# Scores over all 128 rows, sums of the first and last up units made in DRAM, and 192 keys and queries for 256 in the first mixer's tiles

## The reference, cut to what matters

```python
proj = rms_norm(h) @ w_in              # q, k, v of mixer A (16 heads, 4 kv heads) and of mixer B (16 heads)
# mixer A: a 64-token chunk of queries sees its own chunk of keys and the one before (window 128),
#          with a fixed bias by distance and one learned sink logit a head
# mixer B: a chunk sees its own and the 8 before it (here: every earlier token), with a learned bias
sc = einsum(qc, kb) * dh ** -0.5 + bias;  p = softmax(sc);  o = einsum(p, vb)      # dh = 64
h = h + (sigmoid(gates_a) * (att_a @ w_branch_a) + sigmoid(gates_b) * (att_b @ w_branch_b)) @ w_out
u = square(relu(rms_norm(h) @ w_mlp_in))          # w_mlp_in: 2048 x 8192
h = h + u @ w_mlp_out                             # w_mlp_out: 8192 x 2048
out = rms_norm(h)
```

## Time and profile before

| | us |
|---|---|
| median of three runs (2509.68 to 2511.41) | 2510.68 |
| the profiled execution | 2511.8 |
| its span, first to last instruction | 2510.0 |
| PE busy | 2483.1 (99%) |
| PE weight loads busy | 2186.5 (87%) |
| DVE busy | 1674.0 (67%) |
| ACT busy | 1024.6 (41%) |
| POOL busy | 195.6 (8%) |

### The profile page before, as it was taken

One profiled execution on the slowest core, in us unless ns is written; L12 is line 12 of the kernel. 1 busy time (PEld: TensorE's weight loads), 2 busy tenths in 40 slices (PEclk: granted clock), 3 DMA queues, 4 the chain that ended last, 5 costly groups with the idle time before them and its releaser, 6 DMA issues.

```text
span 2510.0 us, 34657 instructions
## 1 busy us (share of the span) xinstructions
PE 2483.1 (99%) x14226; PEld 2186.5 (87%) x14226; DVE 1674.0 (67%) x2280; ACT 1024.6 (41%) x1316; POOL 195.6 (8%) x178
## 2 busy tenths in 40 slices
PE   9999999999999999999999999999999999999998
PEld 8898888888888888878899999999997888888886
DVE  5566555556333332524688888888889888877897
ACT  5455654456222222312444333333335444444445
POOL 0000000000101000001200000000011011110010
PEclk9999999999999999999999999999999999999999
DMA  7777777777889989842233434334348666566652
GB/s 258 212 214 193 216 195 200 215 200 214 235 253 245 266 239 253 259 150 93 76 126 127 134 127 135 127 131 138 128 158 331 230 227 212 197 229 234 228 192 109
DMA packets 192225, 483.54 MB, mean 193 GB/s; under 512 B 13104, under 2 KB 117696, under 8 KB 182224
## 3 DMA queue, kind: packets, MB, share of 16 engines
q1 hardware_dynamic: 180672, 347.26, 41.2%
q0 software_dynamic: 11264, 134.23, 21.4%
q10 hardware_dynamic: 144, 0.02, 0.0%
HBM read 460.44 MB, written 155.23 MB: 245 GB/s over the span
## 4 chain that ended last, share of the span: by engine, by line
PE 95%; DVE 2%; DMA 2%; POOL 1%; issue 0%; ACT 0%; SPq 0%; DVEq 0%; POOLq 0%; ACTq 0%
PE bank L1576 30%; PE bank L1578 30%; PE bank L1577 30%; PE bank L1654 2%; PE bank L1683 1%; PE bank L1666 1%; DMA landing<-in_w_out 1%; POOL raw_forms L1473 0%; DMA landing<-in_w_in 0%; DVE form_lo_b L1257 0%; DMA raw_forms<-hidden_rows 0%; DVE at_lo L1144 0%; DVE up_lo L1289 0%; PE bank L1583 0%; DMA up_raw<-in_up_units 0%
## 5 line engine op out<-in xcount | busy, mean ns | idle before, releaser
L941 DVE TENSOR_TENSOR w_lo<-landing,w_hi 128x1024 fp32r<-128x1024 f32 x200 | 248.8, 1244 | 469.7 <-ACT w_hi L613 469.3
L613 ACT ACTIVATE w_hi<-landing 128x1024 fp32r<-128x1024 f32 x200 | 212.1, 1060 | 626.3 <-PE bank L1578 612.5
L824 ACT ACTIVATE up_hi<-up_raw 128x1792 fp32r<-128x1792 f32 x128 | 218.1, 1704 | 413.1 <-PE bank L1578 392.3
L1576 PE MATMUL bank<-xn_hi,w_hi 128*128 128x512 f32 x928 | 367.0, 395 | 3.1 <-DVE w_lo L941 2.5
L871 ACT ACTIVATE ring<-down_raw 128x1024 fp32r<-128x1024 f32 x224 | 237.5, 1061 | 310.7 <-PE bank L1578 310.7
L1578 PE MATMUL bank<-xn_hi,w_lo 128*128 128x512 f32 x928 | 361.8, 390 | 0.0
L1577 PE MATMUL bank<-xn_lo,w_hi 128*128 128x512 f32 x928 | 361.4, 389 | 0.0
L1370 DVE TENSOR_TENSOR ring<-down_raw,ring 128x1024 fp32r<-128x1024 f32 x224 | 285.4, 1283 | 68.2 <-ACT ring L871 68.2
L1289 DVE TENSOR_TENSOR up_lo<-up_raw,up_hi 128x1792 fp32r<-128x1792 f32 x128 | 262.2, 2048 | 75.7 <-ACT up_hi L824 75.7
L1576 PE MATMUL bank<-ring,down_forms 128*128 128x512 f32 x656 | 255.4, 389 | 2.4 <-DVE ring L1370 2.4
L1576 PE MATMUL bank<-form_hi_b,up_hi 128*128 128x256 f32 x896 | 254.0, 283 | 3.5 <-DVE up_lo L1289 3.5
(11 more groups left out here) (180 smaller groups left out, 4809.4 us busy)
## 6 DMA issues: line engine op xcount, KB each, us to landing
down_totals<-in_down_blocks POOLq DMA_DIRECT2D x64, 1024.0 KB, 8.7
up_raw<-in_up_units SPq DMA_DIRECT2D x128, 512.0 KB, 3.4
down_raw<-down_totals SPq DMA_DIRECT2D x128, 512.0 KB, 4.5
down_raw<-in_down_blocks SPq DMA_DIRECT2D x96, 512.0 KB, 4.3
landing<-in_w_in SPq DMA_DIRECT2D x72, 512.0 KB, 5.8
landing<-in_w_gate SPq DMA_DIRECT2D x64, 512.0 KB, 6.0
landing<-in_w_out SPq DMA_DIRECT2D x32, 512.0 KB, 3.7
hidden_rows<-hidden_out SPq DMA_DIRECT2D x32, 512.0 KB, 3.4
```

Of the source, the lines that this page charges most:

```text
L613: nc.scalar.activation(w_hi[:, u % SPLIT, :], landing[:, u % LAND, :], ACT.Copy).then_inc(unit_hi, 1)
L824: nc.scalar.activation(up_hi[n % 2], up_raw[n % 3][:, 1:8, :], ACT.Copy).then_inc(up_hi_done, 1)
L941: nc.vector.tensor_tensor(w_lo[:, s, :], landing[:, u % LAND, :], w_hi[:, s, :].bitcast(F32), ALU.subtract).then_inc(unit_lo, 1)
L1576: nc.tensor.matmul(dst, a_hi, b_hi, start=start, stop=False, **kw)
```

## The change

**1. Scores.** The low queries are doubled like the high ones, and both groups of `scores` run over 128 rows (the product low by low comes with it). `double_q` makes four copies for two, waits for `proj_ready` (the low queries, made by DVE) in place of `proj_hi`, and there is one buffer for both parts in place of two buffers of the high part.

**2. Tiles of mixer A.** A 128-query tile sees 192 keys: tile t > 0 takes keys 128t - 64 to 128(t+1). `scores`, the bias step, the exponential and the normalising work on 192 for 256. `turn_probs` still turns two blocks of 128 (the unseen 64 columns are zeroed once). `times_v` multiplies each key block with 192 queries for 256.

**3. Up sums.** For the first eight and the last eight up units the sums are made in DRAM, by two more steps of `totals` (18 for 16), which run first; the first ten steps follow each other by 8 units for 10. SP loads the four ready blocks of such a unit with a second DMA of 512 KB, in rows of 1 KB. `up_sums` on POOL is gone, and on DVE for these units.

In the diff `UP_END` is 8 and `UP_UNITS` 128.

```diff
+def summed_in_dram(n):
+    return n < UP_END or n >= UP_UNITS - UP_END
...
 def head_tiles(h):
-
+    if h < A_HEADS:
+        places = ((4, 0), (4, P), (5, 0), (5, 2 * P))
+        return [(max(0, t * P - CHUNK), P + CHUNK * (t > 0), *places[t], 2 * P * t - (P - CHUNK) * (t > 0))
+                for t in range(TT)]
...
+def turned_keys(h, t):
+
+    return P * (1 + (t > 0)) if h < A_HEADS else P * (t + 1)
...
+        def q_parts(h):
+            return (q_hi[:, 0, :], q_lo[:, 0, :]) if h >= HEADS - 4 else (q_twice[:, 0, :], q_twice[:, 1, :])
...
+                if summed_in_dram(n):
+                    end = int(n >= UP_END)
+                    if n in (0, UP_UNITS - UP_END):
+                        sp.wait_ge(totals_added, 16 * 4 * (end + 1))
+                    sums = up_totals[end, :, :, n - end * (UP_UNITS - UP_END), :]
+                    sp.dma_start(up_raw[n % 3][:, 4:8, :], sums.rearrange("b p n -> p b n"))\
+                        .then_inc(up_landed[n % 3], 16)
...
             def double_q(h):
-                act.wait_ge(proj_hi, ready_count(block_no("q", mixer, g)))
-                if h >= 2:
-                    act.wait_ge(scores_done, h - 1)
+                act.wait_ge(proj_ready, ready_count(block_no("q", mixer, g)))
+                if h:
+                    act.wait_ge(scores_done, h)
                 r, qb = q_place(h)
-                nc.scalar.activation(q_twice(h)[0:DH], q_hi[r:r + DH, qb, :].bitcast(F32), ACT.Copy)
-                nc.scalar.activation(q_twice(h)[DH:P], q_hi[r:r + DH, qb, :].bitcast(F32), ACT.Copy).then_inc(q_doubled, 1)
+                for twice, part in zip(q_parts(h), (q_hi, q_lo)):
+                    for half in range(2):
+                        ins = nc.scalar.activation(twice[half * DH:(half + 1) * DH], part[r:r + DH, qb, :].bitcast(F32), ACT.Copy)
+                ins.then_inc(q_doubled, 1)
...
             def up_high(n):
-                if n in (1, 2, 3):
-                    act.wait_ge(up_summed_first, 3 * n)
+                if summed_in_dram(n):
+                    act.wait_ge(up_landed[n % 3], up_landings(n))
                 else:
-                    act.wait_ge(up_summed, 3 if n == 0 else 3 * (n - 2))
+                    act.wait_ge(up_summed, 3 * (n - UP_END) + 3)
...
-                if n + 2 < UP_UNITS:
+                if not summed_in_dram(min(n + 2, UP_UNITS - 1)):
                     up_sums(n + 2)
...
-            for m in range(STEPS):
-                pool.wait_ge(unit_used, 12 + 10 * m)
+            for m in range(2 + STEPS):
+                pool.wait_ge(unit_used, 12 + 8 * m if m < 10 else 84 + 10 * (m - 9))
...
             def scores(h):
-                for rows, query in ((slice(0, P), q_twice(h)), (slice(r, r + DH), q_lo[r:r + DH, qb, :])):
+                for k, query in enumerate(q_parts(h)):
                     for t, (first, n, bk, col, _) in enumerate(head_tiles(h)):
                         ins = nc.tensor.matmul(bank[:, bk, col:col + n], query[:, t * P:(t + 1) * P],
-                                               keys[rows, first * P:first * P + n],
-                                               start=col == 0 and query.shape[0] == P, stop=query.shape[0] == DH,
+                                               keys[:, first:first + n], start=col == 0 and k == 0, stop=k == 1,
                                                skip_group_check=True)
```

More of the change, by code:

```diff
@@ L40 @@
             + [(SUBS - 2 + s, v) for s, v in IN_TURN])
+UP_END = len(IN_TURN)
 UP_FORM = (0, 3, 5, 1, 4, 2, 6)
@@ L87, in up_place, with up_landings @@
     return UP_ORDER.index((s, v))
+def summed_in_dram(n):
+    return n < UP_END or n >= UP_UNITS - UP_END
+def up_landings(n):
+    return 16 * sum(2 if summed_in_dram(k) else 1 for k in range(n % 3, n + 1, 3))
 def form_places():
@@ L302, in q_place, with turned_part @@
             return hh % 2 * DH, 2 * (g % 2) + hh // 2
+        def turned_part(part, h, t):
+            if h >= A_HEADS:
+                return part[:, t, 0:P * (t + 1)]
+            if t == 0:
+                return part[:, 0:1, 0:P]
+            at = 512 * (t - 1) + P
+            return part[:].rearrange("p t n -> p (t n)")[:, at:at + 768].rearrange("p (b n) -> p b n", n=384)[:, :, 0:P]
         def block_parts(c):
@@ L682, in turned_probs @@
                     act.wait_ge(pt_done, TT * h + bank_end(h, t))
-                    nc.scalar.activation(pt_hi[:, t, first * P:first * P + n], bank[:, bk, col:col + n], ACT.Copy)\
+                    turned = bank[:, bk, col:col + turned_keys(h, t)]
+                    if h < A_HEADS:
+                        turned = turned.rearrange("p (b n) -> p b n", n=P)
+                    nc.scalar.activation(turned_part(pt_hi, h, t), turned, ACT.Copy)\
                         .then_inc(pt_hi_done, 1)
@@ L1074, in turned_probs @@
                     dve.wait_ge(pt_hi_done, TT * h + bank_end(h, t))
-                    nc.vector.tensor_tensor(pt_lo[:, t, first * P:first * P + n], bank[:, bk, col:col + n],
-                                            pt_hi[:, t, first * P:first * P + n].bitcast(F32), ALU.subtract)\
+                    turned = bank[:, bk, col:col + turned_keys(h, t)]
+                    if h < A_HEADS:
+                        turned = turned.rearrange("p (b n) -> p b n", n=P)
+                    nc.vector.tensor_tensor(turned_part(pt_lo, h, t), turned, turned_part(pt_hi, h, t).bitcast(F32),
+                                            ALU.subtract)\
                         .then_inc(pt_lo_done, 1)
@@ L1279, in up_sums @@
                     .then_inc(up_summed, 1)
-                before = 0 if n == 0 else 3 * (n - 3)
+                before = 3 * (n - UP_END)
                 dve.wait_ge(up_summed, before + 1)
@@ L1491, in totals @@
             def totals(m, part):
-                blocks, sums = down_blocks[m // 2, m % 2], down_totals[m // 2, m % 2]
+                if m < 2:
+                    blocks, sums = up_ends[m], up_totals[m]
+                else:
+                    step = m - 2
+                    blocks, sums = down_blocks[step // 2, step % 2], down_totals[step // 2, step % 2]
                 def copied(src, dst):
@@ L1662, in turn_probs @@
                     pe.wait_ge(const_landed, 16)
+                    pe.wait_ge(unseen_zero, 1)
                 for t, (_, n, bk, col, at) in enumerate(head_tiles(h)):
                     pe.wait_ge(probs_ready, TT * h + t + 1)
-                    for k in range(n // P):
+                    keys = turned_keys(h, t)
+                    start = at + n - keys
+                    for k in range(keys // P):
                         ins = nc.tensor.transpose(bank[:, bk, col + k * P:col + (k + 1) * P],
-                                                  probs[:, at + k * P:at + (k + 1) * P], identity[:])
+                                                  probs[:, start + k * P:start + (k + 1) * P], identity[:])
                     ins.then_inc(pt_done, 1)
@@ L1679, in times_v @@
                 for j in range(TT):
-                    last = min(j + 2, TT) if h < A_HEADS else TT
-                    dst = bank[:, PV_BANK, j * P:last * P].rearrange("p (t q) -> p t q", q=P)
+                    if h < A_HEADS:
+                        n = P + CHUNK * (j < TT - 1)
+                        dst = bank[:, PV_BANK, j * P:j * P + n]
+                    else:
+                        dst = bank[:, PV_BANK, j * P:].rearrange("p (t q) -> p t q", q=P)
                     for part in (pt_hi, pt_lo):
-                        ins = nc.tensor.matmul(dst, v_parts[:, s, j, head, :],
-                                               part[:, j:last, j * P:(j + 1) * P],
+                        moving = part[:, j, 0:n] if h < A_HEADS else part[:, j:TT, j * P:(j + 1) * P]
+                        ins = nc.tensor.matmul(dst, v_parts[:, s, j, head, :], moving,
                                                start=j == 0 and part is pt_hi,
@@ L1872 @@
                         axis=3).reshape(SUBS, 4, P, 4 * CB)
+    up_ends = np.stack([np.stack([up_units[s, v].reshape(P, 4, CB)[:, (1, 0, 3, 2)] for s, v in part], axis=2)
+                        .transpose(1, 0, 2, 3) for part in (UP_ORDER[:UP_END], UP_ORDER[-UP_END:])])
     w_down = inputs["w_mlp_out"].reshape(CHUNKS, 4, 2, P, 2, 2, QC)
```

41 lines of the change are left out of this document (12 added, 29 removed).

## The result

| | before | after |
|---|---|---|
| median of four runs on the same chip, us | 2510.18 (2508.76 to 2511.41) | 2496.35 (2493.94 to 2497.18) |
| the profiled execution, us | 2511.8 | 2495.8 |
| its span, us | 2510.0 | 2493.9 |

The account below looks back on a forecast made before the run. PE, busy 99% of the span, was taken as the bound. Terms summed to -12.2 us, from 2511.8 to 2499.6; the median lying 1.1 below the profiled run made it 2498.5, range 2489 to 2508.

Parts of the forecast that it names:

- scores over 128 rows: Scores in all heads: the gaps around the second group, over 64 rows, go; -15.5 us (ends 0 and 15.8).
- 192 for 256: Mixer A's times_v and scores: 192 matmuls get shorter, bounded by weight loads 0.113 us apart; -1.3 us.
- wait ahead of head 0: Before head 0's scores: PE stands still for four copies of the low queries; +2.5 us.
- slow clock behind it: After the wait ahead of head 0: PE at 1.2 GHz for part of 5 us; +1.6 us, 0 as other end.
- waits for copies in later heads: Heads 2, 10, 12 and 14: PE waits for the two further query copies; +1.4 us (0 to 3).
- output projection: Output projection's weights: the last step of totals begins later and overlaps their already late loads; +1.0 us (0 to 4).
- start of the up product: First up units: waits and slow clock of 6.5 us shrink to two waits of 0.85; -4.8 us (3 to 6.5 off).
- end of the up product: Last up units: extra 512 KB loads ahead of the hidden blocks delay POOL and DVE's form part; +2.0 us (0 to 3.4).
- by columns: Rival: 192-wide matmuls come at 0.093 us, no short copy waits, clock holds after head 0; 2491.5 us, chance 0.10.
- the gaps stay: Rival: gaps in scores come from the weights' source or tile order, not 64 rows; 2514.0 us, chance 0.04.
- late transfers: Rival: last step of totals costs 4, hidden blocks 3.4, and the clock falls there (1.6); 2504.5 us, chance 0.06.
- slower: Rival: the scores stage becomes bound by transfers during the ten steps of totals; 2516 us or over, chance 0.04.

Follow-up runs that it names:

- the second experiment: Changed kernel with the second group of scores over 64 rows again, all else kept: 2509.01 us, ratio 0.9999 to the kernel before.
- The experiment with the gates: Changed kernel with ACT's copies of the queries ahead of a gate block's sigmoid where both fall into one stage: 2495.16 us, ratio 0.9942.
- the last experiment: Kernel of all four edits, with the input's four loads issued one by one between the output projection's weight units: 2489.29 us, ratio 0.9914.

## Why the prediction was right

Forecast 2498.5, measured 2496.35 (2497.33 on another chip), by the mechanism named: the second group of `scores` no longer stands off from the first. That the sum came so near is in part luck, as the terms show. The scores gave 3.3 less than forecast; the two ends of the up product together cost 3.0 less (0.5 of this comes back in the tail); and an output projection that happened to be 3.4 shorter, for 1.0 longer, is in the trace on top of that. Term by term, forecast against the profiled traces:

| term | forecast | measured |
|---|---|---|
| scores over 128 rows | -15.5 | -12.2 |
| 192 for 256 | -1.3 | -1.8 |
| wait ahead of head 0 | +2.5 | +2.7 |
| slow clock behind it | +1.6 | +1.7 |
| waits for copies in later heads | +1.4 | +1.3 |
| transposes in mixer B | +0.9 | +1.0 |
| output projection | +1.0 | -3.4 (chance) |
| start of the up product | -4.8 | -6.2 |
| end of the up product | +2.0 | +0.4 |
| start and tail of the program | 0 | +0.8 |
| sum | -12.2 | -15.7 (of 16.0) |

**Scores.** The switch of rows was the cause, as the second experiment shows: 11.0 net, which is about 12.2 less the 1.0 that the transposes take back. The size was off by a fifth, and the step that was mis-sized is the comparison: `times_v` was taken as what `scores` would come to. But `scores` have a 128-wide tile ahead of a wide one twice, which costs 0.05 each, and `times_v`, where the two 128-wide ones stand side by side at the end, has none. It is so in both mixers: 1.33 stayed in head 17, where 1.22 was forecast, and in the kernel with tiles of 256 `scores` of head 1 take 0.98, where 0.89 was forecast. Mixer B gained 0.40 a head for 0.51, mixer A 0.365 for 0.48 apart from the tiles.

**192 for 256.** The bound was the weight load: 0.113 in this trace. It gave 1.8, by the experiment with tiles of 256, so 0.11 a head where 0.08 was forecast; the rival by columns (5.2) was not seen. The Trainium skill (TensorE: Matmul & The Clock Gate, LDWEIGHTS (loading the stationary operand)) has columns/1.2 for a load, by which 128 columns come to an estimated 107 ns, and the trace agrees with that to 6 ns.

**Head 0.** PE stood still for 2.57 where 2.5 was forecast, and the clock fell as forecast, though that needn't have happened (see the last section). Both were shown by taking them away (4.0 us in the traces, 4.4 in the medians).

**Later heads.** Heads 2, 10, 12 and 14 wait 0.10, 0.20, 0.46 and 0.46 beyond the usual 0.11, and head 4, not foreseen, 0.07. The experiment with the gates removed the last two.

**Transposes.** 0.09 in eleven heads and nothing in the other five, as forecast (0.08 in eleven).

**Output projection.** This term failed: +1.0 was forecast, and the trace has -3.4. The wait was there before (ACT's wait of 9.51 in the earlier trace rows, which left PE idle for 2.15 with a slow clock behind it), and with SP's four loads of the input in a row it is there in every trace of the changed kernel and its variants, from 0.1 to 3.5 of idle time for PE, though the change does nothing there but move the last step of totals. So +1.0 was well inside what one execution differs from another by, and the -3.4 is no merit of the change that these runs could show. What makes the weights late stays open between SP's four loads ahead of them, for which the last experiment speaks, and the last step of totals, which was put down: no kernel had the loads in a row with the totals out of the way, or the reverse.

**Start of the up product.** The forecast left two waits of 0.85 from start to start against 5.04 of PE; one of 0.80 came, of which 0.52 is idle. DVE had the first 0.8 in hand when the first of its two long stretches began: unit 3 took 5.14, within 0.1 of the pace, and unit 4 took 5.81; before, units 2 to 4 took 7.51, 7.33 and 7.33, part of that at the slow clock. With the slow clock gone too that makes 6.2.

**End.** The chain SP, POOL, DVE did move, by 0.9 against PE, and a wait of PE for DVE on the way became 0.4 shorter. The 3.4 from issue to landing of one DMA, of which 2.0 was taken, was the wrong price; the runs show 0.7 to 0.9. That the loads overlap and only a part of one delays the next is the likely reason, but it isn't shown.

Of the rivals, "by columns" had no short waits for the copies and no slow clock, but they are there; "the gaps stay" is refuted by head 17; of "late transfers" the hidden blocks cost 1.0 for 3.4 and the clock held there (the down product took 610.81 in both traces), while its 4 for the last step of totals can't be told from the wait that was there already; "slower" shows nowhere: the stages of the heads got shorter and the one from the branches to the output projection stayed at 0.0, with the steps of totals closer together.

**Open.** From PE's last matmul to the end it takes 12.55 before, 13.1 after, and again 12.55 and 12.57 in the two kernels with the rear sums on DVE. So this 0.5 belongs to the rear sums too, which makes their whole price 1.0 against the kernel before and 1.3 against the one with the front sums alone; by what way it gets there was not found.

## What to carry to other kernels

When PE is 99% busy, compare from start to start matmuls of equal columns under unlike conditions, and include their neighbours on both sides: the row that stands out (here 64 of 128 rows) is where time lies. Doubling an operand to keep one shape of the array gave 11 us for 56 more copies on an engine that was 41% busy, and 5.7 of it went again where a copy stood between the operand and its user (2.7 and the slow clock of 1.7 at head 0, 1.3 in later heads). Letting head 0 keep the old form brought 4 back. A difference in one stage between two profiles that the change doesn't touch deserves a second profile before it is explained.

## What the runs showed of the hardware

- The second group over 64 rows cost 0.40 a head in mixer B beyond its columns, at four places: 0.094 on the last matmul ahead of it (0.329 for 0.235), 0.104 on its first (0.163 for 0.059), 0.092 on its last (0.325 for 0.233) and 0.107 on the product behind (0.339 for 0.232). The Trainium skill (TensorEngine Tiling (Array Packing), Key Properties) says that a change of tiling mode makes the array drain; the trace agrees that each change has a price, here 0.2, spread over the two matmuls at the border; that it is a drain, no row shows.
- After the same 2.57 of idle time the clock did not always do the same. From 91 to 95 it was 0.57 in after. In its repeat it fell later, and from head 0 to head 1 it cost as much (15.13 for 15.11):

```profile
91.00:95.00 4.00, 4.00 (x17) 3.40 (x18) 2.49 (x10) 3.53 (x8) 0.00 (x0) 0.70 1.02 184
95.00:99.00 4.00, 4.00 (x16) 3.16 (x16) 1.31 (x6) 0.67 (x4) 0.00 (x0) 0.87 1.01 208
```

In the kernel with the sums on DVE, which is the same program up to there but for the steps of totals, it stayed at 1.00:

```profile
91.00:95.00 4.00, 4.00 (x22) 3.48 (x23) 2.49 (x10) 3.53 (x8) 0.00 (x0) 1.00 1.06 217
```

Nine traces have this idle time. From head 0 to head 1 one of them takes 13.5 (nothing lost), six take 15.1 to 15.4 (1.6 to 1.7 lost, apart from the slower scores of the kernel over 64 rows), and two take 16.5 and 16.6 (3.0 to 3.1 lost). The price of such a stretch is a chance, most often 1.6 here, and no fixed term.
- A 128-wide matmul that stands behind a wide one takes 0.06 to the next, and the next one takes 0.05 longer than others of its width. The two together come to 0.23 where the second has 256 columns (0.059 and 0.171), which is two weight loads of 0.113.
